# State updates, routing exponentials and recurrence set-up moved in a two-layer decoder step

## The chip, the cores and the metric

The kernel runs on one core of a Trainium2 chip. Its engines work side by side and are ordered by semaphores: TensorE (PE, with its weight loads shown as PEld), VectorE (DVE), ScalarE (ACT), GpSimd (POOL) and SyncE (SP), which here only issues loads. The metric is the device time of one execution in microseconds, the median of the timed runs.

## The reference, cut to what matters

Two groups of tokens, a prompt of 256 tokens and 8 sequences of 4 tokens (288 columns together), pass through a trunk of two layers with width 1024.

```python
for i in range(2):
    hm = rms_norm(x) * (1 + sc1) + sh1                  # shift, scale, gate from cond @ ada_w
    mixed = gla_mixer(hm) if i == 0 else rglru_mixer(hm)
    x = x + g1 * mixed
    hm = rms_norm(x) * (1 + sc2) + sh2
    x = x + g2 * peer_mixer(hm)
y = rms_norm(x)

# gla_mixer: per chunk of 64 tokens (per sequence of the samples)
S = S * exp(b_end) + k_end^T v ;  o = scores v + qd S

# rglru_mixer: hs[t] = a[t] * hs[t-1] + b[t]
a  = where(reset, 0, exp(log_a)) ; mult = where(reset, 1, sqrt(1 - a*a))
b  = mult * gate_i * xconv ;       out = (hs * gelu(y)) @ w_out

# peer_mixer: 8 heads, two scores over 128 keys each, top 16 of each, top 16 of 256 sums
g = softmax(best) ; wgt = g * gelu(u_tab[idx] . x) ; out = sum(wgt * v_tab[idx])
```

The two tables of the channel mixer (peer_mixer) have 128 x 128 rows of width 1024 per layer.

## The kernel before, in words

**Split products.** A product in full precision is made of three: each weight chunk of 128 x 1024 is loaded into one of four slots of `raw`, a high part `w_hi` is made of it (ScalarE, `high`, L732) and a low part `w_lo = raw - w_hi` (VectorE, `low`, L1693, or GpSimd, L548). TensorE multiplies high by high, high by the activations' low part, and low by high (L1167 to L1169, or `u_high` L1296, L1297 and `u_low` L1301). `w_hi` and `w_lo` have two slots. SP loads the next chunk into a slot when the low part made from it is done. ScalarE makes the high part of chunk c once TensorE has finished chunk c - 2.

**Order.** It is written out by hand: each engine has its own program, and the instructions of one engine run in the order written. Semaphores count finished pieces (`hi_done`, `lo_done` for VectorE's low parts, `lo_pool` for GpSimd's, `split_used` for chunks that TensorE has finished, `pu_evac` for results taken out of PSUM).

**First mixer (0 to some 230 us).** 24 chunks of input projection (j = 0 to 23); the pieces of the attention are put between them (`gla_piece` on TensorE, `gla_step` on VectorE, `gate_step` on ScalarE). VectorE makes the low part of chunk j and then does `gla_step(j)`. At j = 20 to 22 it updates the states of samples 0 to 2, at j = 23 those of samples 3 and 4 (`state_sample`, L1774: four instructions of 128 x 256 each). TensorE makes the products for samples 3 and 4 at j = 21 (L1472). Behind chunk 22 it waits until the states of samples 0 to 4 are done (`stn_ready`) and then transposes the attention's outputs (L1550, sixteen; L1555, two) into the banks that held these products; chunk 23 follows.

**Channel mixer (from some 290 us in layer 0, 1362 us in layer 1).** Routing is VectorE's: `route` for tokens 0 to 127, 128 to 255 and the 32 sample tokens. A route finds the best 16 of each score and of the sums (L1796 to L1802), subtracts the best (L1860, `shift_ready`), turns positions into numbers (L1870 to L1874, 128 x 2048), waits for ScalarE's exponentials (`softmax_exp`, L843, `exp_ready`) and divides by their sum (L1876 to L1878). TensorE transposes the result (`turn_slots`). Beside it, TensorE multiplies the first 64 of 128 chunks of the u table (`u_early`, EARLY = 64). GpSimd makes the low parts of the first POOL_LOWS = 56 of them, VectorE, behind its routing, the rest. Then come 64 late chunks with the one-hot products of the routing, and 128 chunks of the v table. ScalarE's exponentials are written behind chunks 26, 39 and 52 in layer 0 and behind 27, 39 and 51 in layer 1, whose chunks run in hardware loops of four; ScalarE's function table is loaded anew between exp and gelu. In layer 0, further chunks of the conditioning matrix are put between the chunks (`ada_step`).

**Recurrent mixer (some 1157 to 1298 us).** 20 input chunks, then gates, sigmoid and exponentials. VectorE makes high and low part of chunks 15 to 19 (L2215 and L1693), `recur(0)` behind chunk 18 and `recur(1)` behind chunk 19. `recur` (L2192) is: `(a + 1) * mult` (L2198), two memsets, a wait for GpSimd's gated input (`gx_ready`, L666), the product with it (L2202), the carried-in state (L2204, L2205), a memset and the scan (L2208). GpSimd then multiplies five tiles of the result with gelu(y) (L670), and the output projection starts on them.

Of the kernel before, what the change touches and what calls it, by code (L numbers as in the profile page):

```python
# [20 lines left out]
ALU = mybir.AluOpType  # L21
# [22 lines left out]
EARLY = NKEY - LATE  # L44
POOL_LOWS = 56
PICKS = PH // 4 * TOPK
GRING = 3
# [114 lines left out]
def build_step(nc, xt, ct, par, con, ada, gla_in, w_lr, w_gate2, gla_out, wq, keys, u_tab, u_rows, v_tab, rg_in, gates,  # L162
               rg_out, rg_tail, gla_state, h_state, conv_state,
               y_out, gla_p_out, gla_s_out, h_out, conv_p_out, conv_s_out):
    with ExitStack() as ctx:
# [519 lines left out]
        def _(act):  # L685
# [125 lines left out]
            def peer(lay):  # L811
# [132 lines left out]
                if lay == 0:  # L944
                    for c in range(EARLY):
                        u_early_ada(c)
                        if c in (26, 39, 52):
                            softmax_exp((26, 39, 52).index(c))
                    for n in range(LATE):
                        u_late_ada(n)  # L950
                else:
                    u_early(0, True)
                    for first, last, tt in ((1, 7, 0), (7, 10, 1), (10, 13, 2), (13, 16, None)):
                        with act.Fori(first, last) as i:
                            u_early(i, False)
                        if tt is not None:
                            softmax_exp(tt)
                    u_late(0, True)
                    with act.Fori(1, LATE // 4) as i:
                        u_late(i, False)  # L960
# [174 lines left out]
            rg_evac(17)  # L1135
            rg_evac(18)
            full_out = (STREAM["rg_out"] // RING + 1) * 16
            act.wait_ge(lo_done, LOWS["rg_in"] + 20)
# [22 lines left out]
        def _(pe):  # L1161
# [91 lines left out]
            def peer(lay):  # L1253
# [82 lines left out]
                if lay == 0:  # L1336
                    for c in range(EARLY):
                        ada_step(c, pm[:, 2, :], pm[:, 3, :])
                        u_early(0, c, c < POOL_LOWS)
                        if c in (27, 47):  # L1340
                            turn_slots((27, 47).index(c))
                    pe.wait_ge(mod_ready, 8)
                    pe.wait_ge(sel_ready, 1)
                    for n in range(LATE):
                        ada_step(EARLY + n, pm[:, 0, :], pm[:, 1, :])
                        u_late(0, n, n < 4)
                else:
                    for first, last, tt in ((0, 7, 0), (7, 13, 1)):
                        with pe.Fori(first, last) as i:
                            for s in range(4):  # L1350
                                u_early(i, s)
                        turn_slots(tt)
                    for c in range(52, EARLY):
                        u_early(c // 4, c % 4, c < POOL_LOWS)
                    for s in range(4):
                        u_late(0, s, True)
                    with pe.Fori(1, LATE // 4) as i:
                        for s in range(4):
                            u_late(i, s, False)
# [310 lines left out]
        def _(dve):  # L1670
# [386 lines left out]
            def gla_step(j):  # L2057
# [56 lines left out]
                if j == 22:  # L2114
# [7 lines left out]
                    stt(o_root, o_tmp, 1.5, o_root, ALU.add, ALU.mult).then_inc(oinv_ready, 1)  # L2122
                if j == 23:
                    state_sample(3, pm[:, 0:2, :])
                    state_sample(4, pu[:, 2:4, :])

            for j in range(2, 24):
# [64 lines left out]
            def recur(half):  # L2192

                tiles = slice(half * HALF, half * HALF + HALF)
                a, m, xi, h = av[:, tiles, :], mult[:, tiles, :], g_i[:, tiles, :], g_r[:, tiles, :]
# [4 lines left out]
                link(dve.memset(m[:, :, 0:1], 1.0))  # L2200
                dve.wait_ge(gx_ready, HALF * half + HALF)
                link(tt_(m, m, xi, ALU.mult))  # L2202
                a0, b0, h_in = samples(a)[:, :, :, 0], samples(m)[:, :, :, 0], h0[:, tiles, :]
                link(tt_(h_in, a0, h_in, ALU.mult))  # L2204
                link(tt_(b0, b0, h_in, ALU.add))  # L2205
                link(dve.memset(a0, 0.0))
# [4 lines left out]
            for c in range(15, 20):  # L2211
# [5 lines left out]
                if c == 18:  # L2217
                    recur(0)
# [126 lines left out]
```

## Time and profile before

| | |
|---|---|
| timed runs | 2188.91, 2189.32, 2189.34 us (median 2189.32) |
| profiled execution | 2193.3 us, span 2191.5 us |
| TensorE busy | 2095.8 us, 96% |
| VectorE busy | 1570.7 us, 72% |
| ScalarE busy | 1376.9 us, 63% |
| GpSimd busy | 998.1 us, 46% |
| loads and stores | 459.91 MB, mean 210 GB/s |

The page gives the span in 40 slices of 54.8 us. Each digit is the busy share in tenths; PEclk is the granted clock of TensorE, 9 standing for 90% and more:

```profile
PE   6998899999999999999998889898999999999998
DVE  3436573896888887878768554949788887777875
ACT  2534444546888877767754634456788886776774
POOL 1010047787888732223302300888888883222330
PEclk8999999999999999999999999999999999999999
```

A row in order of time has the start in us, the duration, the engine, the line of the program, the operation, the tiles (out<-in) with their shape, and how many equal instructions it stands for. Behind it, in brackets, is the time that the engine had been idle before it and what ended that.

### The profile page before, as it was taken

To read this page: it belongs to the slowest core of one execution; us is meant where nothing else is said; L and a number is where in the kernel's file an instruction comes from. 1 tells how busy PE (TensorE), PEld (TensorE's weight loads), DVE (VectorE), ACT (ScalarE), POOL (GpSimd) and SP (SyncE) were. 2 spreads that over 40 slices of the span, in tenths; PEclk is the share of its full clock that TensorE was granted. 3 is DMA by queue.
4 is the path that set the end of the run, shared out by engine and by line. 5 is a ranking of instruction groups with operands and counts; after the bars stand their busy time and mean duration, and the time that the engine had idled before them with its cause. 6 is when DMAs were issued, how large, how long until landed. Compare 5 with 4: busy or idle time off the path is not lost.

```text
span 2191.5 us, 42211 instructions
## 1 busy us (share of the span) xinstructions
PE 2095.8 (96%) x14238; PEld 1851.8 (85%) x14238; DVE 1570.7 (72%) x2877; ACT 1376.9 (63%) x2502; POOL 998.1 (46%) x841
## 2 busy tenths in 40 slices
PE   6998899999999999999998889898999999999998
PEld 3777898889999987777778789898999998777776
DVE  3436573896888887878768554949788887777875
ACT  2534444546888877767754634456788886776774
POOL 1010047787888732223302300888888883222330
PEclk8999999999999999999999999999999999999999
DMA  9744436666555568888853443454644447888883
GB/s 354 257 152 162 151 122 222 240 223 230 184 189 196 202 221 298 297 306 293 301 196 119 144 138 125 144 184 152 202 135 134 137 140 239 294 294 302 302 293 121
DMA packets 125491, 459.91 MB, mean 210 GB/s; under 512 B 14016, under 2 KB 14544, under 8 KB 124352
## 3 DMA queue, kind: packets, MB, share of 16 engines
q1 hardware_dynamic: 102976, 377.14, 50.7%
q0 software_dynamic: 21504, 79.53, 9.9%
q10 hardware_dynamic: 896, 1.76, 0.2%
q8 instruction: 66, 1.08, 0.2%
q14 instruction: 49, 0.40, 0.1%
HBM read 449.93 MB, written 8.44 MB: 209 GB/s over the span
## 4 chain that ended last, share of the span: by engine, by line
PE 78%; DVE 9%; issue 4%; POOL 4%; ACT 2%; DMA 2%; SPq 0%; DVEq 0%; POOLq 0%; ACTq 0%
PE pm L1369 11%; PE pm L1371 11%; PE pm L1370 11%; PE pu L1301 9%; PE pu L1296 9%; PE pu L1297 8%; POOL w_lo L548 3%; PE pu L1167 3%; PE pu L1168 3%; PE pu L1169 3%; PE pm L1329 3%; PE pm L1330 3%; PE pm L1189 1%; PE pm L1180 1%; DVE arena L1799 1%
## 5 line engine op out<-in xcount | busy, mean ns | idle before, releaser
L1693 DVE TENSOR_TENSOR w_lo<-raw,w_hi 128x1024 fp32r<-128x1024 f32 x492 | 640.0, 1301 | 419.9 <-ACT w_hi L732 339.0
L732 ACT ACTIVATE w_hi<-raw 128x1024 fp32r<-128x1024 f32 x599 | 632.0, 1056 | 440.9 <-PE pm L1371 224.3
L1296 PE MATMUL pu<-hid_hi,w_hi 128*128 128x256 f32 x2048 | 504.7, 287 | 8.0 <-ACT w_hi L732 7.9
L1297 PE MATMUL pu<-hid_lo,w_hi 128*128 128x256 f32 x2048 | 496.1, 281 | 0.0
L1296 PEld LDWEIGHTS pu<-hid_hi,w_hi 128*128 128x128 f32 x2048 | 388.5, 190 | 33.8 <-issue 30.8
L1369 PE MATMUL pm<-w_hi,hid_lo 128*128 128x512 f32 x1024 | 404.1, 395 | 2.2 <-DVE hid_lo L1950 2.2
L1371 PE MATMUL pm<-w_lo,hid_lo 128*128 128x512 f32 x1024 | 402.6, 393 | 0.0
L1370 PE MATMUL pm<-w_hi,hid_lo 128*128 128x512 f32 x1024 | 401.7, 392 | 0.0
L548 POOL TENSOR_TENSOR w_lo<-raw,w_hi 128x1024 fp32r<-128x1024 f32 x112 | 300.1, 2689 | 204.2 <-ACT w_hi L732 203.2
L1297 PEld LDWEIGHTS pu<-hid_lo,w_hi 128*128 128x128 f32 x2048 | 388.4, 190 | 0.0
L1301 PE MATMUL pu<-hid_hi,w_lo 128*128 128x256 f32 x2048 | 295.4, 287 | 16.2 <-POOL w_lo L548 15.6
L1301 PEld LDWEIGHTS pu<-hid_hi,w_lo 128*128 128x128 f32 x2048 | 261.6, 190 | 21.3 <-POOL w_lo L548 20.5
L588 POOL TENSOR_TENSOR oh_lo<-oh_eq,sel_w 128x256 fp32r<-128x256 bf16 x256 | 278.3, 1087 | 0.0
L1167 PE MATMUL pu<-hid_hi,w_hi 128*128 128x288 f32 x736 | 231.7, 315 | 26.6 <-DVE hid_lo L1743 15.9
L1369 PEld LDWEIGHTS pm<-w_hi,hid_lo 128*128 128x128 f32 x1024 | 192.2, 188 | 69.6 <-issue 15.1
L1371 PEld LDWEIGHTS pm<-w_lo,hid_lo 128*128 128x128 f32 x1024 | 192.4, 188 | 43.6
L1168 PE MATMUL pu<-hid_lo,w_hi 128*128 128x288 f32 x736 | 223.2, 303 | 0.0
L1169 PE MATMUL pu<-hid_hi,w_lo 128*128 128x288 f32 x736 | 222.2, 302 | 0.0
L1370 PEld LDWEIGHTS pm<-w_hi,hid_lo 128*128 128x128 f32 x1024 | 192.7, 188 | 33.6
L866 ACT ACTIVATE w_lo<-const,sel_i 128x128 fp32r<-128x128 f32 x512 | 176.2, 392 | 65.7 <-PE pm L1330 65.0
L568 POOL DMA_INDIRECT arena<-in_v_tab,sel_i x64 | 110.1, 1721 | 219.5 <-DVE arena L1976 174.4
L587 POOL TENSOR_TENSOR w_lo<-oh_eq,sel_w 128x256 fp32r<-128x256 bf16 x256 | 160.3, 626 | 95.7 <-PE pm L1330 49.3
(277 smaller groups left out, 3079.4 us busy)
## 6 DMA issues: line engine op xcount, KB each, us to landing
raw<-in_u_tab SPq DMA_DIRECT2D x256, 512.0 KB, 3.5
raw<-in_v_tab SPq DMA_DIRECT2D x256, 512.0 KB, 3.5
raw<-in_ada SPq DMA_DIRECT2D x80, 512.0 KB, 3.6
raw<-in_wq SPq DMA_DIRECT2D x32, 512.0 KB, 3.5
raw<-in_gla_in SPq DMA_DIRECT2D x24, 512.0 KB, 4.7
raw<-in_rg_in SPq DMA_DIRECT2D x20, 512.0 KB, 3.5
arena<-in_ada SPq DMA_DIRECT2D x8, 1024.0 KB, 16.7
arena<-in_gla_state POOLq DMA_DIRECT2D x8, 512.0 KB, 11.1
```

The source lines that it names most:

```text
L548: pool.tensor_tensor(w_lo[:, s % 2, :], raw[:, slot, :], w_hi[:, s % 2, :].bitcast(F32), ALU.subtract).then_inc(lo_pool, 1)
L732: act.activation(w_hi[:, s2, :], raw[:, s4, :], ACT.Copy).then_inc(hi_done, 1)
L1167: mm(out, w_hi[:, s2, cols], r_hi, start=(kk == 0), stop=False)
L1168: mm(out, w_hi[:, s2, cols], r_lo, start=False, stop=False)
L1169: return mm(out, w_lo[:, s2, cols], r_hi, start=False, stop=(stop and kk == n_k - 1))
L1296: mm(pu[:, s, 0:SEQ], w_hi[:, s % 2, kk * P:kk * P + P], hid_hi[:, kk, 0:SEQ], start=(kk == 0), stop=False)
L1297: mm(pu[:, s, 0:SEQ], w_hi[:, s % 2, kk * P:kk * P + P], hid_lo[:, kk, 0:SEQ], start=False, stop=False)
L1301: last = mm(pu[:, s, 0:SEQ], w_lo[:, s2, kk * P:kk * P + P], hid_hi[:, kk, 0:SEQ], start=False, stop=(kk == KD - 1))
L1369: mm(out, hid_lo[:, s, tok], w_hi[:, s % 2, cols], start=start, stop=False)
L1370: mm(out, hid_lo[:, 4 + s, tok], w_hi[:, s % 2, cols], start=False, stop=False)
L1371: last = mm(out, hid_lo[:, s, tok], w_lo[:, s % 2, cols], start=False, stop=stop)
L1693: tt_(w_lo[:, s2 if l2 is None else l2, :], raw[:, s4, :], w_hi[:, s2, :].bitcast(F32), ALU.subtract).then_inc(lo_done, 1)
```

## The change

- First mixer: VectorE does the states of samples 3 and 4 ahead of the low part of chunk 23 instead of behind it.
- Routing: ScalarE's exponentials are behind chunks 14, 32 and 41 in layer 0 and 15, 35 and 47 in layer 1; TensorE's transposes behind 20 and 39, and 19 and 43. POOL_LOWS is 48: VectorE makes the low parts of chunks 48 to 63.
- Recurrence: `recur` is divided. `prepare` has what doesn't need GpSimd's input: L2198, the memsets and L2204. It is done for both halves behind the low part of chunk 18, then `recur(0)`, the low part of chunk 19, `recur(1)`. The high part of chunk 19 is made by ScalarE, behind its copy of tile 17.

```diff
--- before.py
+++ after.py
@@ -42,8 +42,10 @@
 GROUPS = SEQ // 2
 LATE = GROUPS // 2
 EARLY = NKEY - LATE
-POOL_LOWS = 56
+POOL_LOWS = 48
 PICKS = PH // 4 * TOPK
+EXP_AT = (14, 32, 41)
+TURN_AT = (20, 39)
 GRING = 3
 GUSES = [len(range(b, 2 * PICKS, GRING)) for b in range(GRING)]
 
@@ -944,13 +946,13 @@
                 if lay == 0:
                     for c in range(EARLY):
                         u_early_ada(c)
-                        if c in (26, 39, 52):
-                            softmax_exp((26, 39, 52).index(c))
+                        if c in EXP_AT:
+                            softmax_exp(EXP_AT.index(c))
                     for n in range(LATE):
                         u_late_ada(n)
                 else:
                     u_early(0, True)
-                    for first, last, tt in ((1, 7, 0), (7, 10, 1), (10, 13, 2), (13, 16, None)):
+                    for first, last, tt in ((1, 4, 0), (4, 9, 1), (9, 12, 2), (12, 16, None)):
                         with act.Fori(first, last) as i:
                             u_early(i, False)
                         if tt is not None:
@@ -1133,9 +1135,11 @@
             act.wait_ge(pu_evac, BANKED["rg_in"] + 17)
             act.activation(yb[:, 0:7, :], yb[:, 0:7, :], ACT.Gelu_apprx_tanh).then_inc(gelu_y, 1)
             rg_evac(17)
+            act.wait_ge(lo_done, LOWS["rg_in"] + 19)
+            at, full = rg_load("w", 19)
+            high(at, 1, full)
             rg_evac(18)
             full_out = (STREAM["rg_out"] // RING + 1) * 16
-            act.wait_ge(lo_done, LOWS["rg_in"] + 20)
             high(0, 0, full_out)
             rg_evac(19)
             act.wait_ge(split_used, SPLIT["rg_out"])
@@ -1337,20 +1341,20 @@
                     for c in range(EARLY):
                         ada_step(c, pm[:, 2, :], pm[:, 3, :])
                         u_early(0, c, c < POOL_LOWS)
-                        if c in (27, 47):
-                            turn_slots((27, 47).index(c))
+                        if c in TURN_AT:
+                            turn_slots(TURN_AT.index(c))
                     pe.wait_ge(mod_ready, 8)
                     pe.wait_ge(sel_ready, 1)
                     for n in range(LATE):
                         ada_step(EARLY + n, pm[:, 0, :], pm[:, 1, :])
                         u_late(0, n, n < 4)
                 else:
-                    for first, last, tt in ((0, 7, 0), (7, 13, 1)):
+                    for first, last, tt in ((0, 5, 0), (5, 11, 1)):
                         with pe.Fori(first, last) as i:
                             for s in range(4):
                                 u_early(i, s)
                         turn_slots(tt)
-                    for c in range(52, EARLY):
+                    for c in range(44, EARLY):
                         u_early(c // 4, c % 4, c < POOL_LOWS)
                     for s in range(4):
                         u_late(0, s, True)
@@ -2120,11 +2124,11 @@
                     link(tt_(o_tmp, o_root, o_root, ALU.mult))
                     link(stt(o_tmp, o_tmp, -0.5, o_mean, ALU.mult, ALU.mult))
                     stt(o_root, o_tmp, 1.5, o_root, ALU.add, ALU.mult).then_inc(oinv_ready, 1)
+
+            for j in range(2, 24):
                 if j == 23:
                     state_sample(3, pm[:, 0:2, :])
                     state_sample(4, pu[:, 2:4, :])
-
-            for j in range(2, 24):
                 low(SPLIT["gla_in"] + j, mix_load("w", j)[0], j % 2)
                 gla_step(j)
                 if j in MIX_MODS:
@@ -2189,33 +2193,43 @@
                     conv_tile(c - 3)
                 if c == 2 + RT:
                     dve.engine_nop().then_inc(conv_vec, 1)
-            def recur(half):
+            def halves(half):
 
                 tiles = slice(half * HALF, half * HALF + HALF)
-                a, m, xi, h = av[:, tiles, :], mult[:, tiles, :], g_i[:, tiles, :], g_r[:, tiles, :]
+                a, m = av[:, tiles, :], mult[:, tiles, :]
+                return a, m, samples(a)[:, :, :, 0], samples(m)[:, :, :, 0], g_i[:, tiles, :], g_r[:, tiles, :], h0[:, tiles, :]
+
+            def prepare(half):
+
+                a, m, a0, _, _, _, h_in = halves(half)
                 dve.wait_ge(exp_a_ready, HALF * half + HALF)
                 dve.wait_ge(sqrt_ready, half + 1)
                 link(stt(m, a, 1.0, m, ALU.add, ALU.mult))
                 dve.memset(a[:, :, 0:1], 0.0)
                 link(dve.memset(m[:, :, 0:1], 1.0))
+                link(tt_(h_in, a0, h_in, ALU.mult))
+                link(dve.memset(a0, 0.0))
+
+            def recur(half):
+
+                a, m, _, b0, xi, h, h_in = halves(half)
                 dve.wait_ge(gx_ready, HALF * half + HALF)
                 link(tt_(m, m, xi, ALU.mult))
-                a0, b0, h_in = samples(a)[:, :, :, 0], samples(m)[:, :, :, 0], h0[:, tiles, :]
-                link(tt_(h_in, a0, h_in, ALU.mult))
                 link(tt_(b0, b0, h_in, ALU.add))
-                link(dve.memset(a0, 0.0))
                 flat = "p a t -> p (a t)"
                 dve.tensor_tensor_scan(h.rearrange(flat), a.rearrange(flat), m.rearrange(flat), 0.0, ALU.mult,
                                        ALU.add).then_inc(h_ready, 1)
 
-            for c in range(15, 20):
+            for c in range(15, 19):
                 at, full = rg_load("w", c)
                 dve.wait_ge(raw_full[at], full)
                 dve.wait_ge(split_used, m0 + c - 1)
                 dve.tensor_copy(w_hi[:, c % 2, :], raw[:, at, :]).then_inc(hi_done, 1)
                 rg_low(c)
-                if c == 18:
-                    recur(0)
+            for half in range(2):
+                prepare(half)
+            recur(0)
+            rg_low(19)
             recur(1)
             low(SPLIT["rg_out"], 0, 0)
             dve.wait_ge(h_ready, 2)

```

## Rows read from the trace of the kernel before

**Rows 1.** The page, its chain of waits: share of the span by engine

```profile
PE 78%; DVE 9%; issue 4%; POOL 4%; ACT 2%; DMA 2%; SPq 0%; DVEq 0%; POOLq 0%; ACTq 0%
```

**Rows 2.** Stages view: window, its length, busy us of each engine, clock, DMA share, GB/s

```profile
168.00:232.00 64.00, 53.64 (x346) 49.03 (x346) 40.44 (x92) 27.32 (x49) 5.16 (x10) 0.92 0.51 175
```

**Rows 3.** Order of time, TensorE, 176 to 192 us: start, duration, engine, line

```profile
176.52 1.03 PE L1472 MATMUL pu<-arena 32*128 32x256 f32 x8
...
180.64 0.29 PE L1169 MATMUL pu<-hid_hi,w_lo 128*128 128x288 f32 x1
...
185.92 1.97 PE L1550 MATMUL pm<-const,arena 128*128 128x128 f32 x8 [4.98 <-DVE arena L1774]
...
189.67 0.59 PE L1167 MATMUL pu<-hid_hi,w_hi 128*128 128x288 f32 x1
...
191.56 0.29 PE L1169 MATMUL pu<-hid_hi,w_lo 128*128 128x288 f32 x1
```

**Rows 4.** Order of time, VectorE, 181 to 186 us

```profile
181.51 1.23 DVE L1693 TENSOR_TENSOR w_lo<-raw,w_hi 128x1024 fp32r<-128x1024 f32 x1 [6.44 <-ACT w_hi L732]
...
184.22 1.65 DVE L1774 SCALAR_TENSOR_TENSOR arena<-arena,pu 128x256 f32<-128x256 f32 x4
```

**Rows 5.** Chain of waits in order of time, 1126 to 1129 us: start, duration, work

```profile
1126.85 1.70 PE pu L1382 x16
```

**Rows 6.** Order of time, VectorE, routing of layer 0 and of layer 1

```profile
392.48 0.29 DVE L1876 TENSOR_REDUCE arena<-arena 128x8 f32<-128x128 f32 x1 [41.91 <-ACT arena L843]
...
1455.94 0.28 DVE L1876 TENSOR_REDUCE arena<-arena 128x8 f32<-128x128 f32 x1 [32.43 <-ACT arena L843]
```

**Rows 7.** Chain of waits in order of time, 490 to 500 us

```profile
493.02 0.95 PE pu L1301 x8
...
495.83 0.95 PE pu L1301 x8
```

**Rows 8.** Order of time, GpSimd, 1454 us

```profile
1454.03 2.39 POOL L548 TENSOR_TENSOR w_lo<-raw,w_hi 128x1024 fp32r<-128x1024 f32 x1 [0.42 <-ACT w_hi L732]
```

**Rows 9.** Order of time, ScalarE, routing of both layers

```profile
433.14 1.38 ACT L717 ACTIVATE mod<-pm,parm 128x9 f32<-128x9 f32 x8
...
1416.44 1.06 ACT L732 ACTIVATE w_hi<-raw 128x1024 fp32r<-128x1024 f32 x1 [1.50 <-PE pu L1301]
...
1495.49 0.31 ACT L843 ACTIVATE arena<-arena 128x128 f32<-128x128 f32 x1 [3.74 <-DVE arena L1860]
...
1533.56 1.28 ACT L843 ACT_TABLE_LOAD   x1
1534.85 0.23 ACT L843 ACTIVATE arena<-arena 128x32 f32<-128x32 f32 x1
...
1546.95 1.28 ACT L732 ACT_TABLE_LOAD   x1 [1.55 <-PE pu L1301]
```

**Rows 10.** Order of time, TensorE, first matmuls of chunks 39 to 41, layer 1

```profile
1491.74 0.28 PE L1296 MATMUL pu<-hid_hi,w_hi 128*128 128x256 f32 x1
...
1498.31 0.38 PE L1296 MATMUL pu<-hid_hi,w_hi 128*128 128x256 f32 x1 [3.59 <-ACT w_hi L732]
...
1502.77 0.28 PE L1296 MATMUL pu<-hid_hi,w_hi 128*128 128x256 f32 x1
```

**Rows 11.** Chain of waits in order of time, 1549 to 1554 us

```profile
1550.83 1.15 DVE w_lo L1693
```

**Rows 12.** Order of time, GpSimd, recurrent mixer

```profile
1232.60 0.79 POOL L666 TENSOR_TENSOR arena<-arena 128x288 f32<-128x288 f32 x1 [29.42 <-ACT arena L1108]
...
1237.17 2.14 POOL L666 TENSOR_TENSOR arena<-arena 128x288 f32<-128x288 f32 x1
```

**Rows 13.** Order of time, VectorE, recurrent mixer

```profile
1229.81 1.65 DVE L2198 SCALAR_TENSOR_TENSOR arena<-arena 128x1440 f32<-128x1440 f32 x1
...
1236.50 2.17 DVE L2202 TENSOR_TENSOR arena<-arena 128x1440 f32<-128x1440 f32 x1 [4.89 <-POOL arena L666]
```

**Rows 14.** Order of time, TensorE, start of the recurrent mixer's output projection

```profile
1257.67 0.58 PE L1167 MATMUL pu<-hid_hi,w_hi 128*128 128x288 f32 x1 [7.36 <-DVE hid_lo L2233]
```


## The prediction

> **What bounds the kernel now.** I read the page first: TensorE ends the chain of waits for 78% of the span, VectorE for 9%, GpSimd for 4% [rows 1]. So only time in which TensorE stands still, or runs at its lower clock, can be won. The busy table shows where that is: in 168 to 232 us TensorE is busy 53.6 of 64 us at a granted clock of 0.92 [rows 2], and the page's slices show the same dips around 1200 and 1400 us. Then I read the order of time in four places, with the idle time written behind the instruction that ended it: the end of the first mixer [rows 3, 4], the routing of both layers [rows 6 to 11], and the end of the recurrent mixer [rows 12 to 14]. The reader should see in each who was late, and whether that engine had been idle itself.
>
> **First mixer (the two states ahead of low part 23).** Chunk 22 issues its last matmul at 180.64. The transposes behind it wait 4.98 us for VectorE's state updates (L1774) and start at 185.92 [rows 3]. VectorE had been idle for 6.44 us: it stood in front of the low part of chunk 23, for whose high part ScalarE comes late, at 181.51, and did the states of samples 3 and 4 behind it, four updates in 1.65 us for each state, the second from 184.22 [rows 4]. What the states read was ready at 176.52 + 1.03 = 177.55 [rows 3]. With the states first, even if both began only there, they end by 177.55 + 2 x 1.65 = 180.85, ahead of 180.93, when chunk 22 ends. The 4.98 us go, less some 0.1 us of issue. The low part of 23 still starts at 181.51 and ends at 182.74.
>
> The clock comes on top. The 18 transposes take from 185.92 to 189.67, 3.75 us [rows 3]; sixteen of the same shape take 1.70 us where TensorE has not paused [rows 5], so 18 need 1.9, and 1.85 us are lost to the 1.2 GHz level after the pause. The next eight steps of chunk 23, 189.67 to 191.56, took 1.89 us [rows 3]; 288 columns at 2.4 GHz are 0.12 us, about 0.13 with issue, so they cost 0.8 us too much. Without the pause the transposes end at 181.0 + 1.9 = 182.9, just behind the low part of 23 (182.74), so nothing is late next there. Further on, the gated products, ScalarE's copy of tile 23 and the first low part of the output projection all follow chunk 23 and shift with it; GpSimd's state stores only start earlier, and no one waits for them before the routing. Sum: 4.9 + 1.85 + 0.8 = 7.5 us. Bounds: 5.0 (the clock stays down) and 7.7.
>
> **Routing, layer 0.** VectorE is idle for 41.91 us before 392.48, since ScalarE takes the first exponentials only behind chunk 26 [rows 6]. Behind chunk 14 they would be asked for at about 348, and VectorE's sums end at 392.48 - 41.91 = 350.6, so VectorE runs on. That makes VectorE early and nothing else: TensorE is paced here by its own 2.81 us a chunk (493.02 to 495.83 [rows 7]) and by the low parts on GpSimd, and chunks 48 to 55 have no stall in the trace, whoever makes their low parts. Handing eight of them to VectorE frees GpSimd some 8 x 2.81 = 22 us sooner for its memsets, which were hidden too. VectorE would end the routing some 40 us sooner, at about 449, and chunk 48 comes at about 466: cover of 17 us. What can change is where VectorE's large products collide with GpSimd's low parts. GpSimd needs 2.4 us for a low part left alone [rows 8], up to twice that in a collision; VectorE's part does not shrink, it falls on chunks 27 to 32 instead of 39 to 43. One collision goes: ScalarE did the bias (1.38 us at 433.14 [rows 9]) and a table load (1.28 us, as any [rows 9]) back to back ahead of the next high part, because exponentials 2 and the bias fell on the same chunk 39; now they are on 32 and 39. I take 1 us of gain; bounds -1.5 and 3, since a moved collision can cost as much as one low part's delay.
>
> **Routing, layer 1.** Here VectorE idles 32.43 us for the first exponentials [rows 6], then runs without a pause to the end, and is late twice. First, ScalarE asks for the second exponentials before VectorE has the scores, waits 3.74 us [rows 9], and the high part of chunk 40 queues behind it: TensorE stands 3.59 us and works on at the lower level. The starts are 1491.74 (chunk 39), 1498.31 (40) and 1502.77 (41) [rows 10]: 11.03 us for two chunks that need 5.63, so 5.4 us. Second, the low part of chunk 56 comes at 1550.83 + 1.15 [rows 11], 0.5 us late. After the change the first exponentials follow chunk 15, whose high part starts at 1416.44 [rows 9]; they are done near 1419.4, ahead of VectorE's sums (1455.94 - 32.43 = 1423.5). VectorE is 32 us earlier from there. The scores of the second half are ready at 1495.4 - 32.4 = 1463, and ScalarE reaches chunk 35 only at about 1478: no wait, and the 5.4 us go.
>
> Two things come back. The loops behind the first exponentials load a table twice per pass, 1.28 us each (one stands before a pass's first high part at 1546.95 [rows 9]). That makes the first low part of a pass late: high part 1.06, low part 2.4 [rows 8], so 0.1 + 1.28 + 1.06 + 0.1 + 2.4 = 4.94 us against 2.81 + 1.88 = 4.69 when TensorE needs it (1.88 is two thirds of a chunk, its 16 matmuls on the high part), 0.25 us of idle and with its ripple 0.25 to 0.6 us. Before, seven passes with low parts on GpSimd stood behind the first exponentials, one of them inside the big stall; after, eight (chunks 16 to 44). I take 1.0 us. And VectorE now waits for the third exponentials behind chunk 47, which come some 3.0 us after TensorE starts chunk 46 (0.1, high part 1.06, gelu 0.3, load 1.28, exponentials 0.23). Weights, ids, selections and first one-hots took it 6.8 us before (1544.0 to 1550.8), of which three waits for GpSimd were some 3.0; I count 3.8 with at most one short wait, since GpSimd's last low part ends then, and 1.2 for the low part of 48: 8.0 us, needed at 2 x 2.81 + 1.88 = 7.5. So 0.5 to 1.5 us of stall at chunk 48 takes the place of the one at 56: 0.2 us net. Sum 5.4 - 1.0 - 0.2 = 4.2; bounds 2 and 6.
>
> A load shows 1.28 us from 1533.56, and the exponentials start right behind it, at 1534.85 [rows 9]. The Trainium skill, "ScalarE: Activation LUTs", section "What ACT_TABLE_LOAD costs", adds a drain of about 1.38 us to every switch, 2.66 us in all. This trace doesn't show the drain; by the page the added passes and chunk 48 would cost an estimated 1.4 us each instead of some 0.5, and the layer would gain 2 to 3 us.
>
> **Recurrent mixer.** TensorE stands 7.36 us before the output projection at 1257.67 [rows 14], for VectorE's chain: first half, copy and low part of chunk 19, second half. VectorE itself waits 4.89 us for GpSimd before 1236.50 [rows 13]. The change fills that gap with the first product of both halves (1.65 us at 1229.81 [rows 13]) and the small ones, and gives the copy of chunk 19 to ScalarE. Out of the chain go 1.65 to 2.25 us of product, 0.7 of state product and 1.2 of copy, 3.9 at most. But the two engines exclude each other: GpSimd's product takes 0.79 us alone and 2.14 us when VectorE's is running [rows 12], VectorE's 2.17 us [rows 13]. The second half's product, from 1232.1, holds GpSimd's first product (1232.60) up to 1233.75, and GpSimd's fifth, on which the first half waits, ends at about 1237.5 instead of 1236.4. Followed on: first scan ends 1244.2 (+0.3); ScalarE has the high part of 19 at 1245.8, behind its gelu; low part ends 1247.5, TensorE starts chunk 19 0.8 us late, which the gap absorbs; GpSimd's five gating products, done by 1252.6 before, now fall into the second half's product and scan and cost these 0.6 us twice and the next low part 0.6. The projection starts at about 1256.4: 1.3 us. Bounds: -1 (each of the five collides) and 3.2 (none does).
>
> **Sum.** 7.5 + 1 + 4.2 + 1.3 = 14.0 us. The profiled execution took 2193.3 us (span 2191.5), so it would take 2179.3; it lies 4.0 us above the median of the timed runs, 2189.3, and the same saving there gives 2175.3 us.
>
> **Rivals.** (a) The routing gives nothing back: the wait at chunk 40 returns as low part 48 and table loads. Speaks for it: VectorE's readiness is tied to exponentials at chunk 47. Against: that is a shift of about 1 us, not 5. Price 4.2 + 1: 2180.5. (b) The pause in the first mixer goes, the lower clock stays, for instance because the short idle times around it do: 7.5 - 5.0 = 2.5 us less, 2177.8. Against: the matmuls up to 180.64 are at full rate (0.29 us) after shorter pauses. (c) Collisions are milder than counted, recurrence 3.2 and layer 0 3: 2171.4. (d) It doesn't do what it says in the first mixer, the states staying last behind a wait I have not seen: 2182.8. (e) Slower: VectorE becomes the bound of the early chunks. With 48 low parts on GpSimd, the routing must end 8 x 2.81 = 22.5 us sooner than before. If the early exponentials didn't bring VectorE forward, layer 1 would stop at chunk 48 for 22.5 + 0.5 = 23 us: 2175.3 + 23 = 2198. It decides from 14 us of lateness on. For it speaks that VectorE is already last at 1550.83 [rows 11]; against it that 32.43 us of idle time are there to take [rows 6].
>
> **Numbers.** Forecast 0.62 (its own range 2171 to 2179.5), (a) 0.17, (b) 0.08, (c) 0.08, (d) 0.02, (e) 0.03. A change of under 0.2%, 4.4 us, can't be told from none. All cases but (e) are beyond it, (d) narrowly; blurring that a little: faster 0.94, same 0.03, slower 0.03. The range for 8 in 10 runs from (c) and the upper bounds of the terms to (a): 2169.5 to 2181.5.
>
> **What would show it.** First mixer: the idle time before L1550 under 0.3 us and its transposes at 0.11 us each. Routing: no idle time of VectorE before its sums in half 0, no wait of ScalarE for L1860, no wait of TensorE at chunk 40, a wait of about 1 us at chunk 48 of layer 1. Recurrence: the wait before the projection near 6 us. Wrong would be a wait of several us at chunk 48, an idle time that has only moved to the next instruction, or a lower clock in 181 to 187 us.

## The result: 17 us less, some 15 of them traced to the parts of the change

Timed, the changed kernel takes 2172.06 us (median of 4 runs, 2171.69 to 2174.79) against 2189.33 us; the ratio is 0.9925, with a 95% interval of 0.9914 to 0.9937, that is 16.4 us (13.8 to 18.8). A second set of the same kernel gave 0.9924 [0.9910, 0.9937]. The forecast was 2175.3 us. The profiled executions are further apart than the medians, 2193.3 and 2171.7 us. 7 of these 21.6 us are won where no instruction was changed, as the table below shows; how much of that is chance, and how much comes with the change by way of the clock, stays open in part.

The page of the kernel after, its chain of waits, share of the span by engine: VectorE's share has fallen from 9% [rows 1] to 4%, and GpSimd's has grown from 4% to 6%.

```profile
PE 81%; issue 6%; POOL 6%; DVE 4%; DMA 2%; ACT 1%; SPq 0%; POOLq 0%; DVEq 0%; ACTq 0%
```

**First mixer.** The stages view answers to [rows 2]: 3 us more of TensorE's work fit into the same 64 us. The granted clock of the 64 us is 0.92 in both, since the next stall, of 5.33 us, lies at 224.68 after and at 234.69 before; in 176 to 192 us it is 1.00, and 0.79 before.

```profile
168.00:232.00 64.00, 56.66 (x377) 52.17 (x376) 46.96 (x107) 30.76 (x56) 5.77 (x10) 0.92 0.52 181
```

The order of time, TensorE, answers to [rows 3]: the transposes follow chunk 22 with no idle time, eight of them in 0.88 us, which is 0.11 each; all 18 take 2.04 us instead of 3.75, and the steps of chunk 23 come every 0.13 us at once.

```profile
178.19 0.29 PE L1173 MATMUL pu<-hid_hi,w_lo 128*128 128x288 f32 x1
178.32 1.04 PE L1554 MATMUL pm<-const,arena 128*128 128x128 f32 x8
179.20 1.04 PE L1554 MATMUL pu<-const,arena 128*128 128x128 f32 x8
180.07 0.38 PE L1559 MATMUL pm<-const,arena 128*128 128x128 f32 x2
180.36 0.40 PE L1171 MATMUL pu<-hid_hi,w_hi 128*128 128x288 f32 x1
180.59 0.30 PE L1172 MATMUL pu<-hid_lo,w_hi 128*128 128x288 f32 x1
```

VectorE, against [rows 4]: both states are done before it waits for the high part of chunk 23, and the low part is as late as ever, here still ahead of its use.

```profile
174.37 1.66 DVE L1778 SCALAR_TENSOR_TENSOR arena<-arena,pm 128x256 f32<-128x256 f32 x4 [1.73 <-PE pm L1476]
175.94 1.65 DVE L1778 SCALAR_TENSOR_TENSOR arena<-arena,pu 128x256 f32<-128x256 f32 x4
179.08 1.22 DVE L1697 TENSOR_TENSOR w_lo<-raw,w_hi 128x1024 fp32r<-128x1024 f32 x1 [1.49 <-ACT w_hi L734]
```

The margin is thin. In a second profile of the changed kernel TensorE reaches the transposes 1.5 us sooner, and then waits for this low part ahead of chunk 23, so that it wins nothing by it. Two of the kernels below, e9 and e10, show the same wait.

```profile
182.03 0.40 PE L1171 MATMUL pu<-hid_hi,w_hi 128*128 128x288 f32 x1 [1.40 <-DVE w_lo L1697]
```

**Routing, layer 1.** The view of waits (who waited for whom: us in all, times, longest) of TensorE over that layer's chunks, of the kernel before and then of the changed one. The 3.6 us for ScalarE are gone; 1.9 us come back as waits for GpSimd and 0.2 for VectorE, at chunk 48; the rest of the gain, some 1.8 us of 3.3, is the clock behind the stall: chunks 39 and 40 took 11.03 us before, 5.4 more than two chunks need, and only 3.59 of these were waiting.

```profile
PE pu L1301 <- POOL w_lo L548: 8.9, 11, 1.3
PE pu L1296 <- ACT w_hi L732: 5.8, 2, 3.6
PE pu L1301 <- DVE w_lo L1693: 0.5, 1, 0.5
```

```profile
PE pu L1305 <- POOL w_lo L550: 10.8, 13, 1.3
PE pu L1300 <- ACT w_hi L734: 2.2, 1, 2.2
PE pu L1305 <- DVE w_lo L1697: 0.7, 1, 0.7
```

In the order of time of the changed kernel, VectorE's sums of the first half run on without idle time, where 32.43 us stood [rows 6]; ScalarE's second exponentials find their scores ready, where it waited 3.74 us [rows 9]; and VectorE waits for the third ones, with TensorE 0.73 us behind it at chunk 48.

```profile
1405.34 0.29 DVE L1880 TENSOR_REDUCE arena<-arena 128x8 f32<-128x128 f32 x1
...
1463.49 1.28 ACT L845 ACT_TABLE_LOAD   x1
1464.78 0.31 ACT L845 ACTIVATE arena<-arena 128x128 f32<-128x128 f32 x1
...
1502.75 0.19 DVE L1880 TENSOR_REDUCE arena<-arena 128x2 f32<-128x32 f32 x1 [3.02 <-ACT arena L845]
...
1507.96 1.22 PE L1305 MATMUL pu<-hid_hi,w_lo 128*128 128x256 f32 x8 [0.73 <-DVE w_lo L1697]
```

**Recurrence.** The order of time, VectorE, against [rows 13]: its wait for GpSimd is down from 4.89 to 2.85 us, for the second half's first product (1215.76) stands in it. The last row is TensorE's: 5.29 us of waiting ahead of the projection instead of 7.36 [rows 14].

```profile
1213.46 1.65 DVE L2207 SCALAR_TENSOR_TENSOR arena<-arena 128x1440 f32<-128x1440 f32 x1
...
1215.76 1.66 DVE L2207 SCALAR_TENSOR_TENSOR arena<-arena 128x1440 f32<-128x1440 f32 x1
...
1221.17 2.17 DVE L2217 TENSOR_TENSOR arena<-arena 128x1440 f32<-128x1440 f32 x1 [2.85 <-POOL arena L668]
...
1224.12 3.65 DVE L2220 TENSOR_TENSOR_SCAN arena<-arena 128x1440 f32<-128x1440 f32 x1
1229.41 1.58 DVE L1697 TENSOR_TENSOR w_lo<-raw,w_hi 128x1024 fp32r<-128x1024 f32 x1 [1.64 <-ACT w_hi L734]
...
1239.81 0.58 PE L1171 MATMUL pu<-hid_hi,w_hi 128*128 128x288 f32 x1 [5.29 <-DVE hid_lo L2247]
```

### The profile page after: what moved, and what is told of

Same layout as the page of the kernel before. It is cut to its first block, busy times and chain, and to the rows that moved or that the text cites. A ratio compares the mean times of both kernels' runs of the same rounds, so it can differ in the third digit from the quotient of the medians.

```text
span 2169.9 us, 42183 instructions
## 1 busy us (share of the span) xinstructions
PE 2082.6 (96%) x14238; PEld 1840.6 (85%) x14238; DVE 1594.4 (73%) x2892; ACT 1385.8 (64%) x2509; POOL 963.3 (44%) x825
## 3 DMA queue, kind: packets, MB, share of 16 engines
q10 hardware_dynamic: 896, 1.76, 0.2%
## 4 chain that ended last, share of the span: by engine, by line
PE 81%; issue 6%; POOL 6%; DVE 4%; DMA 2%; ACT 1%; SPq 0%; POOLq 0%; DVEq 0%; ACTq 0%
PE pm L1373 11%; PE pm L1375 11%; PE pm L1374 11%; PE pu L1305 9%; PE pu L1300 9%; PE pu L1301 8%; POOL w_lo L550 6%; PE pu L1171 3%; PE pu L1172 3%; PE pu L1173 3%; PE pm L1333 3%; PE pm L1334 3%; PE pm L1193 1%; PE pm L1637 1%; DMA arena<-in_ada 1%
## 5 line engine op out<-in xcount | busy, mean ns | idle before, releaser
L1697 DVE TENSOR_TENSOR w_lo<-raw,w_hi 128x1024 fp32r<-128x1024 f32 x508 | 660.1, 1300 | 456.0 <-ACT w_hi L734 373.7
L1300 PEld LDWEIGHTS pu<-hid_hi,w_hi 128*128 128x128 f32 x2048 | 385.7, 188 | 29.0 <-issue 26.6
L550 POOL TENSOR_TENSOR w_lo<-raw,w_hi 128x1024 fp32r<-128x1024 f32 x96 | 263.5, 2756 | 184.2 <-ACT w_hi L734 182.9
```

Of the source, the lines that this page charges most:

```text
L550: pool.tensor_tensor(w_lo[:, s % 2, :], raw[:, slot, :], w_hi[:, s % 2, :].bitcast(F32), ALU.subtract).then_inc(lo_pool, 1)
L1300: mm(pu[:, s, 0:SEQ], w_hi[:, s % 2, kk * P:kk * P + P], hid_hi[:, kk, 0:SEQ], start=(kk == 0), stop=False)
L1697: tt_(w_lo[:, s2 if l2 is None else l2, :], raw[:, s4, :], w_hi[:, s2, :].bitcast(F32), ALU.subtract).then_inc(lo_done, 1)
```

## Experiments

All eleven kernels were timed in 5 rounds beside the kernel before. A single execution lies up to 3.7 us off the median (25 runs of the kernel before: 2184.7 to 2191.9 us), which is as much as most parts are worth, so each experiment is read in two ways: by its ratio, and by where in time the same matmul starts. The table has these starts, from the order of time of TensorE: first the kernel before, then how much earlier (negative) the others are. A part's worth is what a column wins between two lines; what a column wins where its kernel has no change doesn't come from an edit there, and is a measure of what the profiles differ by on their own.

```
matmul                          before   states  routing    recur   before    after    after
                                           only     only     only    again             again
first mixer, before the states  135.51    -0.01    -2.85     0.00    -1.20    -2.43    -0.76
routing 0, chunk 0              302.56    -7.22    -2.29     0.20    -0.93    -9.80    -7.80
routing 0, chunk 2              310.01    -8.24    -3.31     0.25    -0.85   -10.78    -8.82
routing 0, chunk 15             357.33    -9.77    -4.78     0.20    -0.95   -12.34   -10.32
routing 0, chunk 50             476.55    -8.80    -7.42     0.71    -0.84   -14.62   -12.52
before the second mixer        1126.69    -8.95    -7.39     0.61    -1.00   -14.65   -12.65
before the recurrence          1202.16   -11.56    -8.99    -2.00    -0.94   -16.35   -15.27
behind the recurrence          1263.42   -11.85    -8.92    -3.33    -0.88   -18.14   -17.03
routing 1, chunk 10            1402.20   -12.00    -8.92    -3.29    -0.88   -18.20   -16.95
routing 1, chunk 39            1491.74   -12.05    -3.76    -3.33    -0.92   -13.06   -11.80
routing 1, chunk 58            1555.90   -12.01   -12.22    -3.27    -0.88   -21.54   -20.31
last                           2177.99   -12.24   -12.39    -3.20    -1.07   -21.55   -20.25
```

**The three parts alone.** Each is the kernel before with one part of the diff that stands ahead of the prediction: the two `state_sample` lines moved; the constants and loops of the routing; `prepare`, `recur` and ScalarE's copy of chunk 19.

> The kernel before with one part of the change: the states of samples 3 and 4 ahead of the low part of chunk 23 of the first mixer. My theory: the stall of 4.98 us and the lower clock behind it both go, 7.4 us (the profile of after shows 7.4 between the start of the mixer and its end), ratio 0.9966. Rival: the clock does not come back and only the wait goes, 5.0 us, ratio 0.9977. Second rival: part of the 7.4 us is the phase of the run's start and the change is worth under 5.

Measured: 0.9961 [0.9948, 0.9975], 8.5 us (5.5 to 11.4). From the first line to chunk 0 of the routing it wins 7.2 us (after: 7.4). The stall is gone and the transposes start 5.13 us earlier; behind them and eight steps of chunk 23 it is 7.6 us, the clock's share being 2.5. The first theory is right; a clock that stays low is ruled out (granted 1.00 in 176 to 192 us), and so is a worth under 5 us. Seven of the eight profiles with this edit win 7.0 to 7.4 us between these two lines, e10's only 5.8: behind its waits of 1.40 and 1.50 us, at 180.62 and 186.64, the granted clock is 0.63 from 186.6 to 189 us, while e9 with the same two waits keeps 1.00.

> The kernel before with the routing alone changed: 48 low parts on GpSimd instead of 56, exponentials and turns at the new chunks in both layers. The profile of after is 4.8 us shorter in the routing of layer 0 and 4.2 in that of layer 1. Theory: of the 4.8 some 2.5 us are the run's own clock after short pauses, which no part of the change touches, so this kernel gains 4.2 + 2.3 = 6.5 us (ratio 0.9970). Rival A: all 9.0 us are the change's (0.9959). Rival B: the routing gives back what it takes, 0 to 1 us.

Measured: 0.9971 [0.9961, 0.9981], 6.3 us (4.2 to 8.5). From chunk 15 to chunk 50 of layer 0 it wins 2.6 us (after 2.3 and 2.2), where the kernels without a change there lose 0 to 1; from chunk 10 to 58 of layer 1 3.3 us. The 1.0 us before chunk 2 it wins too, ahead of its first change, and the 1.2 us behind chunk 14 the states' kernel wins as well, which has none of these edits. So not all of the 9.0 us are made by these edits, and rival A falls; its ratio, 0.9959, is outside the interval too.

> The kernel before with the recurrence alone changed: first products of both halves before the first half's gating, the copy of chunk 19 on ScalarE. Theory: collisions of VectorE's and GpSimd's products eat more than half of the 3.9 us taken out of the chain; 1.3 to 1.8 us are left (ratio 0.9993). Rival A: no collisions matter, 3.2 us (0.9985). Rival B: nothing is left (1.0000 within 0.0003).

Measured: 0.9994 [0.9985, 1.0003]; by time alone it can't be told from none. Across the recurrence it wins 1.33 us, the whole change 1.79 and 1.76, and the kernels without it 0.3 at most. The theory stands, 3.2 us is out. Before the recurrence, where its instructions are those of the kernel before, it wins 2.6 us, as the states' kernel does too, and the kernel before run again nothing. 1.7 of these stand behind a wait of 1.03 us at 1143.58 (time of before): over the next 6 us the granted clock is 0.72 in before, in its second profile and in e6 (layer 1 alone, below). In all ten other kernels the stretch takes 1.7 us less; the clock there is 1.00 in this kernel and in the changed one. So it isn't simply drawn in each execution; what sets it isn't shown.

> The kernel before once more, unchanged: what two sets of runs of one kernel differ by, and a second profile of it. Expected ratio 1.0000 within 0.0005. Theory: the first matmul of the first mixer, which lies ahead of all changes and was 2.4 us earlier in the profile of after than in that of before, scatters by 1 to 3 us from run to run, and the matmuls behind waits of 2 us of layer 0 (chunks 2, 14, 15) are at times 1.2 us faster or slower in a second profile of the very same kernel. Rival: the second profile repeats the first to 0.2 us in these places; then the 2.4 us and the 2.5 us of layer 0 are not scatter but belong to the changed kernel.

Measured: 1.0004 [0.9995, 1.0013]. The first line scatters as expected (1.2 us, 2.85 in the routing's kernel). The other half was wrong: chunks 2, 14 and 15 of layer 0 repeat the first profile to 0.2 us. They don't do so in any of the nine kernels whose routing starts over 2 us earlier. By the rival's own test the 2.5 us of layer 0 then aren't plain scatter. They may come with the change, since it starts the routing 7 us earlier, and yet they aren't made by an edit of the routing. What sets them stays open.

The ratios of the three parts multiply to 0.9926, against 0.9925 for the whole: within the intervals the parts don't need one another.

**Layer 1 alone, and who makes low parts 48 to 55.**

```
e6: the kernel before, with only
+  for first, last, tt in ((1, 4, 0), (4, 9, 1), (9, 12, 2), (12, 16, None)):   # ScalarE, layer 1
+  for first, last, tt in ((0, 5, 0), (5, 11, 1)):  ...  for c in range(44, EARLY):   # TensorE, layer 1
e5: the changed kernel, with
-POOL_LOWS = 48
+POOL_LOWS = 56
```

> The kernel before with only the exponentials and turns of layer 1 moved (56 low parts on GpSimd, all of layer 0 as before). Theory: the wait of 3.6 us at chunk 40 and the lower clock behind it go, table loads and shifted collisions take some of it: 3.3 to 4.3 us in all (ratio 0.9982), and layer 0 stays as it was to 0.5 us. Rival: the earlier exponentials need the hand-over of eight low parts, without it the wait only moves, 0 to 1 us. The difference to the kernel with the whole routing changed (6.3 us) is then layer 0's, 2 to 3 us, against 1 us in my forecast.

Measured: 0.9979 [0.9970, 0.9988], 4.6 us; in the trace 3.1 us from chunk 10 to 58, and layer 0 is as before to 0.1 us. So the early exponentials carry the gain, and the hand-over isn't needed for it.

> The changed kernel with 56 low parts on GpSimd again instead of 48; exponentials and turns stay at their new chunks. Theory: who makes the low parts of chunks 48 to 55 matters only for VectorE's deadline, which moves from chunk 48 to chunk 56; with VectorE some 10 us early there the wait of 0.73 us at chunk 48 of layer 1 goes, and nothing comes in its place: 0.5 to 1.5 us faster than the changed kernel, ratio to before about 0.9915 to 0.992. Rival: GpSimd's low parts 48 to 55 collide with VectorE's one-hots and the gain is lost, ratio 0.9925 to 0.993; by that the hand-over is worth something by itself.

Measured: 0.9927 [0.9915, 0.9939]. The ratio fits the theory and the rival alike; the trace decides for the rival, with 3.2 us from chunk 10 to 58 against 3.3 in the changed kernel. The wait at chunk 48 is now one of 0.32 us for GpSimd, and a second one of 0.31 us for GpSimd has come behind it. So the hand-over is worth 0.2 us at most. TensorE's row at chunk 48 of this kernel:

```profile
1508.39 1.20 PE L1305 MATMUL pu<-hid_hi,w_lo 128*128 128x256 f32 x8 [0.32 <-POOL w_lo L550]
```

**The third exponentials, and the table loads.**

```
e8: the changed kernel, with
-  ((1, 4, 0), (4, 9, 1), (9, 12, 2), (12, 16, None))
+  ((1, 4, 0), (4, 9, 1), (9, 11, 2), (11, 16, None))
e9: the changed kernel, with, in ScalarE's loops of layer 1
+  if first > 1:
+      u_early(first, False)
+      first += 1
   with act.Fori(first, last) as i:
       u_early(i, False)
e10: both
```

> The changed kernel with the third exponentials of layer 1 behind chunk 43 instead of 47 (and the first passes' split accordingly). Theory: VectorE waits for nothing but these exponentials before chunk 48, so the wait of 0.73 us there and its lower clock go: about 1 us faster than the changed kernel, ratio to before 0.992. Rival: the scores of the second half's last part are not ready at chunk 43, or the exponentials push the high part of chunk 44: no gain or up to 1 us slower.

Measured: 0.9920 [0.9907, 0.9933]; in the trace 3.5 us from chunk 10 to 58 against 3.3, so 0.2 of the 1 us that I expected. The exponentials are there in time, but VectorE now meets GpSimd's low parts (1501.47 to 1504.32 and 1504.28 to 1506.67): two small operations that take 0.48 and 0.18 us in the changed kernel take 1.14 and 2.31, and the wait at chunk 48 is still 0.50 us. Order of time, VectorE, in this kernel:

```profile
1503.03 0.17 DVE L1881 RECIPROCAL arena<-arena 128x2 f32<-128x2 f32 x1
1503.23 1.14 DVE L1882 TENSOR_TENSOR arena<-arena 128x32 f32<-128x32 f32 x1
1504.41 2.31 DVE L1899 TENSOR_SCALAR arena<-arena 128x32 f32<-128x32 f32 x1
1506.74 0.19 DVE L1900 TENSOR_TENSOR arena<-arena 128x32 f32<-128x32 f32 x1
```

> The changed kernel with the first pass of ScalarE's loop behind each group of exponentials of layer 1 written out ahead of the loop, so that the loop is entered with the table of the gelu loaded. Theory: the loops then load no table in their passes (two loads of 1.28 us a pass before; four passes keep theirs), and with them go 0.25 to 0.6 us of TensorE's waits for each of the freed passes, some 8: 2 to 4 us faster than the changed kernel (ratio to before 0.9907 to 0.9916). Rival A: the loads are hidden, waits of TensorE come from GpSimd's collisions with VectorE: 0 to 0.5 us. Rival B: the loads stay in the passes whatever stands ahead of the loop: 0.

Measured: 0.9913 [0.9900, 0.9926]; in the trace 5.3 us from chunk 10 to 58 against 3.3, so 2.0 us more. The grouped view of ScalarE over layer 1 shows what went: first the changed kernel's 25 loads beside gelus and high parts, then the four that are left. With a loop entered behind exponentials, the loads stand in its body and are repeated in every pass; entered behind a gelu it has none, and each written-out pass keeps one. So all twelve passes were freed, not the eight that I counted.

```profile
L836 ACT ACT_TABLE_LOAD x13 | 16.7, 1283 | 0.2
L734 ACT ACT_TABLE_LOAD x12 | 15.4, 1283 | 15.1 <-PE pu L1305 15.0
```

```profile
L836 ACT ACT_TABLE_LOAD x4 | 5.1, 1283 | 0.1
```

> Both edits together: the pass behind each group of exponentials written out, and the third exponentials behind chunk 43. With the passes written out VectorE's sums of the second half ended at 1495.8 and it then waited 6.8 us for the exponentials; asked for four chunks earlier these are ready by then. Theory: the wait at chunk 48 of layer 1 goes entirely (0.44 us with its lower clock 0.6), on top of 2 us of the written-out passes: 2.6 us faster than the changed kernel in the traces, ratio 0.9913, which I would hand in as the best version. Rival: VectorE's small operations collide with GpSimd's low parts as they did when only the exponentials were moved (one took 2.31 us instead of 0.18): 0 to 0.2 us more than with the passes alone.

Measured: 0.9914 [0.9900, 0.9927], median 2170.25 us. In the trace 6.0 us from chunk 10 to 58, 2.7 more than the changed kernel, as expected. VectorE has the selections done before chunk 48 and waits 2.66 us for ScalarE's high part; TensorE doesn't wait at chunk 48. Order of time, VectorE and TensorE:

```profile
1499.91 1.40 DVE L1922 TENSOR_TENSOR oh_eq<-const,sel_i 128x256 bf16<-128x256 f32 x2
1503.97 1.23 DVE L1700 TENSOR_TENSOR w_lo<-raw,w_hi 128x1024 fp32r<-128x1024 f32 x1 [2.66 <-ACT w_hi L734]
...
1504.46 1.11 PE L1308 MATMUL pu<-hid_hi,w_lo 128*128 128x256 f32 x8
```

It is the best version by the traces, 0.7 us in this stretch ahead of the written-out passes alone; the ratio parts it neither from those nor from the changed kernel, since the intervals overlap.

**Only the first half prepared ahead.**

```
-  for half in range(2):
-      prepare(half)
+  prepare(0)
   recur(0)
   rg_low(19)
+  prepare(1)
   recur(1)
```

> The changed kernel with only the first half of the recurrence prepared ahead; the second half's products are prepared behind the low part of chunk 19, as before. Theory: preparing the second half early holds GpSimd up for some 1.1 us but takes 1.65 us and the small operations, 2.2 us, out of the tail: without it the projection starts about 1 us later than in the changed kernel (ratio 0.993). Rival A: the two cancel: 0 to 0.3 us. Rival B: the collision costs more than it saves: this kernel is 0.5 to 1 us faster.

Measured: 0.9936 [0.9923, 0.9950]; across the recurrence 0.1 us instead of 1.8, so 1.7 us lost where 1 was expected. Without the second half prepared ahead nothing of the gain is left. Whether the copy of chunk 19 on ScalarE is needed beside it wasn't tested. The first scan starts at 1223.21, 1.0 us earlier against GpSimd's first product than in the changed kernel, so the collision costs the 1.1 us that I counted. But nothing comes of that microsecond: VectorE stands before the low part of chunk 19 until ScalarE has its high part, 2.65 us instead of 1.64, and then has 2.25 us of product to do in the tail.

```profile
1223.21 3.65 DVE L2220 TENSOR_TENSOR_SCAN arena<-arena 128x1440 f32<-128x1440 f32 x1
1229.51 1.46 DVE L1697 TENSOR_TENSOR w_lo<-raw,w_hi 128x1024 fp32r<-128x1024 f32 x1 [2.65 <-ACT w_hi L734]
1230.90 2.25 DVE L2207 SCALAR_TENSOR_TENSOR arena<-arena 128x1440 f32<-128x1440 f32 x1
```

**The changed kernel again.**

> The changed kernel once more, unchanged: ratio 0.9925 within 0.0007, and a second profile. In three places with nothing of the change before them on the path (first two chunks of layer 0, chunk 14 of layer 0, first chunk of layer 1) the profiles of all kernels with the states ahead gain 0.8, 1.2 and 1.0 us against the profile of before. Theory: it is which short pause the clock happens to drop behind, and follows from where in time the pauses lie, so it repeats in this profile since the kernel is the same. Rival: it is drawn anew in each run, and at least one of the three is missing here.

Measured: ratio as expected. The gains at chunk 2 and chunk 15 repeat, the third doesn't: chunk 0 of layer 1 runs at the lower level this time. The stages view, the same 5.5 us of the same kernel in the first and then in this profile; the column before the last two is the granted clock.

```profile
1354.00:1359.50 5.50, 5.19 (x41) 4.99 (x42) 5.46 (x35) 2.64 (x3) 5.40 (x3) 1.00 0.30 89
```

```profile
1354.40:1359.90 5.50, 5.48 (x33) 5.49 (x34) 5.47 (x35) 1.66 (x2) 4.70 (x2) 0.69 0.28 92
```

So this one differs between executions of one kernel, and the rival holds for it; the other two may follow from the program's own timing.

## Why the prediction was right, step by step

- **First mixer, 7.5 us: right in each term, one of them by luck.** 4.9, 1.85 and 0.8 us were expected; the states' kernel shows 5.13, 1.75 and 0.72 (starts of the transposes, of chunk 23, and of its steps behind the eighth). It helped to price the clock by rows at both levels and not by the length of the pause. But the row that I took for the transposes at full rate, L1382 [rows 5], is not of their shape: its matmuls are 128x32, the transposes 128x128. That sixteen of them take 1.70 us and sixteen transposes 1.75 is luck. "Nothing is late next there" holds in the first profile and fails by 1.40 us in the second. About 0.4 us are given back at 239 us, behind the next stall.
- **Routing, layer 0, 1 us: the term that was mis-sized.** Measured are 2.2 and 2.3 us from chunk 15 to 50 in the changed kernel, 1.4 to 2.6 over all eight kernels with these edits. I counted one collision of ScalarE and called VectorE's collisions with GpSimd a mere move. They do move: the changed kernel loses 3.4 us between chunks 19 and 33 and wins 5.7 between 33 and 50. What I missed is that the sum is not zero: TensorE's waits there fall from five of 3.3 us in all to three of 2.4 us. That is 0.9 of the 2.3 us; the rest is no wait that the view shows. The kernel with 56 low parts wins 2.0 us here, so it is the moved exponentials and turns; no run parts ScalarE's collision from VectorE's.
- **Routing, layer 1, 4.2 us: measured 3.3 and 3.4.** From chunk 39 to 41 the change wins 4.8 us, not 5.4: the two chunks now take 6.2 us and not 5.63, with a short wait for GpSimd of their own. The wait at chunk 48 is 0.73 us (0.5 to 1.5 expected), and VectorE waited for the exponentials there as said. Everything else together costs 1.5 us, where I had 1.2, but not as I had it: 5.1 us are lost between chunks 10 and 39 and 3.7 won between 41 and 58. TensorE's waits for GpSimd's low parts grow from 5.4 to 9.5 us in the first stretch and go from 2.75 to none in the second, as VectorE's sums, and with them its collisions, move forward. Writing the passes out won 2.0 us over twelve passes, 0.17 each and not 0.25 to 0.6; with nine such passes before, the three that were added make an estimated 0.5 us.
- **Recurrence, 1.3 us: measured 1.8** (1.3 when alone). The followed chain was right: from VectorE's first product to the end of the first scan it took 14.3 us (14.4 forecast), to the end of the low part of chunk 19 17.5 (17.7), to the projection 26.35 (26.6). So the projection starts 1.5 us earlier, and 0.3 more is won behind its start. The collision is paid in time in which VectorE would wait for ScalarE anyway.
- **The rest.** The profiles differ by 7 us more than the parts explain (2.4 at the start, 1.0 and 1.5 in layer 0, 1.7 before the recurrence, 1.0 less 0.8 around chunk 0 of layer 1, and small ones). I had carried the saving over to the median unchanged, which leaves out that the profile of before was 4 us above its median. The sum of the causes is 7.4 + 2.3 + 3.3 + 1.8 = 14.8 us, inside the interval of 13.8 to 18.8. With the 2.5 us of layer 0, which my forecast had nothing for, it is 17.3, inside as well, so the timing can't tell whether they belong to the change.
- **Luck in the sum.** 14.8 lies 0.8 us from the 14.0 forecast because the errors of the terms, 1.3 too little in layer 0, 0.9 too much in layer 1 and 0.5 too little in the recurrence, partly cancel. The measured median, 2172.06, lies inside the range but nearer to rival (c)'s 2171.4 than to 2175.3.

Rival (a) is out by the routing alone (6.3 us), (b) by the states alone, (d) by the transposes at 178.32, (e) by layer 1. Of (c), layer 0 came near its 3 us, the recurrence stayed away from 3.2.

The Trainium skill, "ScalarE: Activation LUTs", section "What ACT_TABLE_LOAD costs", adds a drain of about 1.38 us to each switch. The trace doesn't agree: the rows at 1463.49 and 1464.78 above show 1.28 us from the load to the exponentials and no drain; layer 1 gained 3.3 us, not the 2 to 3 that the page's figure gave. The Trainium skill, "SBUF — State Buffer", section "SBUF: two separate sides", says that the pair of ports shared by VectorE and GpSimd is held for a whole instruction by whichever of the two started first. The trace agrees: an operation on 128x32 elements took 2.31 us beside a low part of GpSimd that had started 0.13 us earlier and took 2.39 us, as long as one alone [rows 8], and 0.18 us without it.

## What to carry to other kernels

Work that is ready goes ahead of a wait on the same engine; price what it frees with the clock behind the pause too, from rows at both levels. Before you shorten a step, look at the next wait of the engine that does it: a microsecond won in front of another engine's lateness is worth nothing, and one lost there costs nothing. And a loop on ScalarE that is entered with another function's table loads tables in every pass; one pass written out ahead of each such loop won 2.0 us here, while moving the third exponentials won 0.2.

## What the runs showed of the hardware

- The same program can get another clock behind the same pause: 1.00 or 0.69 over the 5.5 us behind the wait of 2.20 us at chunk 0 of layer 1, worth 1.0 us. A profile's difference of 1 us behind a pause is no effect of a change until a second profile repeats it.
- Two such places, chunks 2 and 15 of layer 0, kept one level in all four profiles whose routing starts within 1 us of the first one's, and the other in all nine whose routing starts over 2 us earlier (granted clock over 4.5 us from chunk 0 on: 0.66 in before, 1.00 in the states' kernel; the wait ahead of it is 2.12 us in both). A third, at 1143.58, parts the kernels 3 to 10. I can't say why.
- Small operations of VectorE (128x32 elements, 0.18 us) take up to 2.42 us when GpSimd's low parts run; moving them to fill an idle time is not free.
